# Experts of a two-layer block: rounds of up to 224 rows, and narrow turns with the rows stationary and the weights moving

## The reference, cut to what matters

```python
def _swiglu(h, w_in, w_out):
    a, b = jnp.split(h @ w_in, 2, axis=-1)
    return (jax.nn.silu(a) * b) @ w_out

def _moe(h, router, w_in, w_out):          # h 512 x 1024, w_in 1024 x 2816, w_out 1408 x 1024, 8 of each
    logits = (h @ router).astype(F32)
    top_v, top_i = lax.top_k(logits, MOE_TOP_K)                    # MOE_TOP_K = 2
    top_w = jax.nn.softmax(top_v, axis=-1)
    gates = jnp.sum(jax.nn.one_hot(top_i, MOE_EXPERTS, dtype=F32) * top_w[..., None], axis=-2).astype(h.dtype)
    return sum(gates[..., e, None] * _swiglu(h, w_in[e], w_out[e]) for e in range(MOE_EXPERTS))
```

## Time and profile before

| | |
|---|---|
| runs | 2776.82, 2778.45, 2781.89 us; median 2778.45 |
| profiled execution, its own time | 2776.83 us |
| its span | 2775.0 us |
| PE busy / DVE / ACT / POOL over the span | 96% / 36% / 24% / 18% |
| a narrow turn (2159.15 to 2221.26 us) | 62.11 us |
| a wide turn (2283.38 to 2400.87 us) | 117.49 us |
| after TensorE's last matmul | 14.90 us |

### The profile page before, as it was taken

The page is one execution under the profiler, slowest core; times in us unless marked ns, Lnnn a source line. Parts: engine busy times, 40 slices in busy tenths (PEclk is TensorE's granted clock), DMA queues, the critical chain, the costliest instruction groups (busy, mean ns, idle before and its releaser), DMA issues. The chain is left out here.

```text
span 2775.0 us, 46116 instructions
## 1 busy us (share of the span) xinstructions
PE 2658.9 (96%) x18752; PEld 1775.5 (64%) x18753; DVE 1003.8 (36%) x2301; ACT 666.8 (24%) x1408; POOL 502.2 (18%) x465
## 2 busy tenths in 40 slices
PE   6999999889999999999999999999988999999997
PEld 3555555555555555556677667766647788677784
DVE  2344454337767763113444444444440110010100
ACT  3344444221222210115232333232111110110110
POOL 0111111022223314222223222321100010000000
PEclk8999999989999999999999999999998999999999
DMA  7224223213333332201001100110239995684831
GB/s 243 67 71 127 68 66 87 82 46 102 110 116 111 106 111 69 63 23 32 20 14 33 32 24 10 32 32 1 70 122 368 334 308 175 204 264 154 267 94 30
DMA packets 321858, 297.60 MB, mean 107 GB/s; under 512 B 5920, under 2 KB 285600, under 8 KB 321568
## 3 DMA queue, kind: packets, MB, share of 16 engines
q1 hardware_dynamic: 315648, 273.17, 32.4%
q0 software_dynamic: 4896, 17.83, 2.5%
q10 hardware_dynamic: 1152, 4.19, 0.4%
HBM read 281.01 MB, written 12.58 MB: 106 GB/s over the span
## 5 line engine op out<-in xcount | busy, mean ns | idle before, releaser
L1762 PE MATMUL bank<-work,weight_ring 128*128 128x128 f32 (+1 forms) x2048 | 317.7, 317 | 1.0 <-ACT work L1812 1.0
L2228 PE MATMUL bank<-hidden,weight_ring 128*128 128x512 f32 (+1 forms) x768 | 308.7, 536 | 1.8 <-ACT work L2572 1.8
L1762 PEld LDWEIGHTS bank<-work,weight_ring 128*128 128x128 f32 x2048 | 291.0, 192 | 24.9 <-ACT work L1812 5.7
L655 PE MATMUL bank<-weight_ring,hidden 128*128 128x384 f32 x760 | 266.7, 495 | 4.8 <-ACT work L799 4.6
L1283 PE MATMUL bank<-hidden,weight_ring 128*128 128x384 f32 x704 | 238.1, 492 | 5.0 <-ACT hidden L426 5.0
L1429 DVE SCALAR_TENSOR_TENSOR weight_ring<-weight_ring,silu_c 128x256 f32<-128x256 f32 x308 | 213.7, 735 | 5.5
L655 PEld LDWEIGHTS bank<-weight_ring,hidden 128*128 128x128 f32 x760 | 138.0, 191 | 109.0 <-ACT work L799 16.6
L1283 PEld LDWEIGHTS bank<-hidden,weight_ring 128*128 128x128 f32 x704 | 133.1, 192 | 93.7 <-issue 7.0
L2228 PEld LDWEIGHTS bank<-hidden,weight_ring 128*128 128x128 f32 x768 | 134.9, 190 | 82.4 <-issue 68.1
L1934 DVE TENSOR_TENSOR work<-work,bank 128x128 f32<-128x128 f32 (+1 forms) x88 | 29.7, 338 | 423.7 <-ACT work L1818 423.7
L1283 PE MATMUL bank<-weight_ring 128*128 128x384 f32 x528 | 182.1, 495 | 0.3 <-DVE work L1437 0.3
(11 more groups left out here) (372 smaller groups left out, 3741.0 us busy)
## 6 DMA issues: line engine op xcount, KB each, us to landing
weight_ring<-in_moe_w_in SPq DMA_DIRECT2D x64, 1024.0 KB, 10.3
weight_ring<-in_ada_w SPq DMA_DIRECT2D x38, 1024.0 KB, 5.3
weight_ring<-in_ffn_w_in SPq DMA_DIRECT2D x44, 512.0 KB, 4.9
hidden<-in_moe_w_out SPq DMA_DIRECT2D x8, 2816.0 KB, 10.6
residual<-in_moe_w_out SPq DMA_DIRECT2D x8, 2816.0 KB, 16.1
work<-in_moe_w_in SPq DMA_DIRECT2D x16, 1024.0 KB, 8.8
weight_ring<-in_na_w_qkv SPq DMA_DIRECT2D x24, 512.0 KB, 8.0
weight_ring<-in_gdn_w_qkv SPq DMA_DIRECT2D x24, 512.0 KB, 5.3
```

The lines of the kernel that those rows point to most:

```text
L655: mm = nc.tensor.matmul(m.psum[6][:, 0:3 * P], m.H[:, k, t * P:(t + 1) * P], weights(u)[:, k, :], start=(k == 0), stop=(k == KD - 1))
L1762: mm = nc.tensor.matmul(B[c % 4][:, ab * HALF:ab * HALF + N], w[:, ab, k, (c % 2) * P:(c % 2 + 1) * P], XG[:, k, 0:N], start=(k == 0), sto ...
L2228: mm = nc.tensor.matmul(B[b][:, c0:c0 + t1 - t0], W[:, s, k, :], m.H[:, k, t0:t1], start=(k == 0), stop=(k == KD - 1))
```

## The change

A round has up to 224 rows in two blocks of 128 and 96, in place of two of 128. The wide turn keeps its form with N = 224. Gather, scatter, transposes, `pick`, `take_rows` and the second product take 96 rows in the second block. 512 tokens now make up to three rounds, so the table has 24 turns (and one) and its last round is cut at the end of the tokens; the extra rounds run if an expert has more than 224 rows.

The narrow turn's first product is turned round. For each slab of 256 hidden units (the last 128), 8 matmuls have the rows `XG[:, k, 0:128]` stationary and move both halves of the slab, 512 columns in two runs of 256. The result has rows on partitions. ScalarE and VectorE work on it a slab at a time, into `sa`, in place. TensorE then transposes each 128 columns back (`turn_back`, eleven a turn, in banks 6 and 7), one slab late, and VectorE copies them to `GT` (`take`).

```diff
-    TURNS = 2 * EXPERTS
     HALF = 2 * P
+    BACK = 96
+    ROUND = P + BACK
+    ROUNDS = -(-LAT // ROUND)
+    TURNS = ROUNDS * EXPERTS
+    BLOCK = (P, BACK)
...
-        with eng.If(most > HALF):
+        with eng.If(most > ROUND):
...
             def scatter(b):
-                nc.gpsimd.indirect_dma_start(out=m.out[0], out_offset=bass.IndirectOffsetOnAxis(ap=row_now[:, b:b + 1], axis=0),
-                                             in_=YS[:, b, :], in_offset=None, compute_op=ALU.add).then_inc(scattered[b], 16)
+                r = slice(0, BLOCK[b])
+                nc.gpsimd.indirect_dma_start(out=m.out[0], out_offset=bass.IndirectOffsetOnAxis(ap=row_now[r, b:b + 1], axis=0),
+                                             in_=YS[r, b, :], in_offset=None, compute_op=ALU.add).then_inc(scattered[b], 16)
...
# TensorE
-            def turn(it, nb):
-                N = nb * P
+            def turn_rows(it, nb):
+                N = sum(BLOCK[0:nb])
...
+            def wide(it):
+                nb = 2
+                N = sum(BLOCK)
+                turn_rows(it, nb)
                 for c in range(EK):
...
+                second(it, nb, ready)
+                pe.sem_inc(turned, SLABS)
+
+            def narrow(it):
+                turn_rows(it, 1)
+
+                def turn_back(j):
+                    pe.wait_ge(gated, it * EK + min(2 * j + 2, EK))
+                    if j < 2:
+                        pe.wait_ge(sum_out, it * 2 + 2)
+                    else:
+                        pe.wait_ge(taken, it * SLABS + j - 1)
+                    for n in range(chunks(j)):
+                        mm = nc.tensor.transpose(B[TURN_BANKS[j % 2]][:, n * P:(n + 1) * P], sa[:, j % 2, n * P:(n + 1) * P], ident)
+                    mm.then_inc(turned, 1)
+
+                for j in range(SLABS):
+                    pe.wait_ge(w_in[j], it * 32 + 32)
+                    if j >= 4:
+                        pe.wait_ge(gated, it * EK + 2 * (j - 4) + 2)
+                    n = width(j)
+                    w = in_slab(j)[:, 0:KD * 2 * n].rearrange("p (s k n) -> p s k n", k=KD, s=2)
+                    for k in range(KD):
+                        if j == 0 and k % 2 == 0:
+                            pe.wait_ge(x_out, it * KD + k + 2)
+                        mm = nc.tensor.matmul(B[j % 4][:, 0:2 * n].rearrange("p (s n) -> p s n", s=2), XG[:, k, 0:P], w[:, :, k, :],
+                                              start=(k == 0), stop=(k == KD - 1))
+                    mm.then_inc(product, chunks(j))
+                    if j == 2:
+                        pick(it + 2)
+                    if j:
+                        turn_back(j - 1)
+
+                def ready(k):
+                    if k == 4:
+                        turn_back(SLABS - 1)
+                    if k % 2 == 0:
+                        pe.wait_ge(taken, it * SLABS + k // 2 + 1)
+
+                second(it, 1, ready)
...
# ScalarE, narrow
+                for j in range(SLABS):
+                    n = width(j)
+                    act.wait_ge(product, it * EK + EK + min(2 * j + 2, EK))
+                    if j >= 2:
+                        act.wait_ge(turned, it * SLABS + j - 1)
+                    nc.scalar.activation(sa[:, j % 2, 0:n], B[j % 4][:, 0:n], ACT.Silu).then_inc(silu_ok, chunks(j))
...
# VectorE, setting up
+            LAST = ROUND * (ROUNDS - 1)
+            for r in range(1, ROUNDS):
+                nc.vector.tensor_scalar(of(2, r), of(2, 0), float(-ROUND * r), None, ALU.add).then_inc(rank_ok, 1)
+            nc.vector.tensor_scalar(late, of(2, 0), float(LAST), None, ALU.is_ge).then_inc(rank_ok, 1)
+            dve.wait_ge(rank_ok, 15)
+            nc.vector.tensor_tensor(of(1, ROUNDS - 1), of(1, ROUNDS - 1), late, ALU.mult).then_inc(rank_ok, 1)
+            nc.vector.tensor_scalar(place, late, float(-LAT), float(LAT), ALU.mult, ALU.add).then_inc(rank_ok, 1)
+            dve.wait_ge(rank_ok, 17)
+            nc.vector.tensor_tensor(of(2, ROUNDS - 1), of(2, ROUNDS - 1), place, ALU.add).then_inc(rank_ok, 1)
...
# VectorE, narrow
+                def take(j):
+                    dve.wait_ge(turned, it * SLABS + j + 1)
+                    nc.vector.tensor_copy(GT[:, 2 * j:2 * j + chunks(j), 0:P], B[TURN_BANKS[j % 2]][:, 0:width(j)].rearrange("p (n t) -> p n t", n=chunks(j)))\
+                        .then_inc(taken, 1)
+
+                for j in range(SLABS):
+                    n = width(j)
+                    dve.wait_ge(silu_ok, it * EK + min(2 * j + 2, EK))
+                    nc.vector.tensor_tensor(sa[:, j % 2, 0:n], sa[:, j % 2, 0:n], B[j % 4][:, n:2 * n], ALU.mult).then_inc(gated, chunks(j))
+                    if j == 0:
+                        next_turn(it)
+                    if j:
+                        take(j - 1)
+                    if j == 3:
+                        next_rows(it)
+                take(SLABS - 1)
+                weighted(it, 1)
```

More of the change, by code:

```diff
@@ L1573, in experts, with chunks, rounds @@
     Y_BANKS = ((5, 6), (7, 5))
+    TURN_BANKS = (6, 7)
     def width(s):
         return HALF if s < SLABS - 1 else P
-    def rounds(eng, turn):
+    def chunks(j):
+        return width(j) // P
+    def rounds(eng, wide, narrow):
         eng.wait_ge(table_ok, 2)
@@ L1584, in rounds @@
             with eng.If(mine > P):
-                turn(e, 2)
+                wide(e)
             with eng.Else():
-                turn(e, 1)
-        with eng.If(most > HALF):
+                narrow(e)
+        with eng.If(most > ROUND):
             with eng.Fori(EXPERTS, TURNS) as it:
-                turn(it, 2)
+                wide(it)
     with nc.Block() as block:
@@ L1680, in _ @@
                 turn(e)
-            with pool.If(most > HALF):
+            with pool.If(most > ROUND):
                 with pool.Fori(EXPERTS, TURNS) as it:
@@ L1766, in turn @@
                         pick(it + 2)
[L1767 to L1779, removed]
@@ L1783, in _ @@
+            rounds(pe, wide, narrow)
         @block.scalar
@@ L1813, in turn, with wide @@
                                              scale=m.MODA[:, 1, 1, 2 * j + k, 0:1]).then_inc(x_out, 1)
+            def wide(it):
+                N = sum(BLOCK)
+                turn_rows(it, 2)
                 for c in range(EK):
@@ L1818, in turn, with narrow @@
                     nc.scalar.activation(sa[:, c % 2, 0:N], B[c % 4][:, 0:N], ACT.Silu).then_inc(silu_ok, 1)
-            rounds(act, turn)
+            def narrow(it):
+                turn_rows(it, 1)
+                for j in range(SLABS):
[4 more added lines that the diff above has]
+                    nc.scalar.activation(sa[:, j % 2, 0:n], B[j % 4][:, 0:n], ACT.Silu).then_inc(silu_ok, chunks(j))
+            rounds(act, wide, narrow)
         @block.vector
@@ L1880, in _ @@
             tok = const(m, C_TOK, 4).unsqueeze(2).broadcast_to([P, 4, EXPERTS])
-            for r in range(2):
+            for r in range(ROUNDS):
                 nc.vector.tensor_copy(of(0, r), tok).then_inc(rank_ok, 1)
@@ L1927, in _, with next_turn, next_rows, weighted @@
             dve.wait_ge(gain_out, 2)
[L1928 to L1944, removed]
+            dve.wait_ge(rank_ok, 19)
+            def next_turn(it):
+                    dve.wait_ge(picked, it + 1)
+                    nc.vector.tensor_copy(now.unsqueeze(2), table[:, :, bass.ds(it + 1, 1), :]).then_inc(now_ok, 1)
+                    dve.wait_ge(now_ok, it + 2)
+                    one_hots()
+            def next_rows(it):
+                    dve.wait_ge(idx_kept, it + 1)
+                    for b in range(2):
+                        dve.wait_ge(gathered[b], it * 16 + 16)
+                    take_rows(it + 2)
+            def weighted(it, nb):
                 for half in range(2):
@@ L1957, in turn, with wide, narrow @@
                 keep_gates(it + 2)
-            rounds(dve, turn)
+            def wide(it):
+                N = sum(BLOCK)
+                for c in range(EK):
+                    dve.wait_ge(silu_ok, it * EK + c + 1)
+                    nc.vector.tensor_tensor(GT[:, c, 0:N], sa[:, c % 2, 0:N], B[c % 4][:, HALF:HALF + N], ALU.mult).then_inc(gated, 1)
+                    if c == 1:
+                        next_turn(it)
+                    if c == 7:
+                        next_rows(it)
+                dve.sem_inc(taken, SLABS)
+                weighted(it, 2)
+            def narrow(it):
+                def take(j):
[7 more added lines that the diff above has]
+                    if j == 0:
+                        next_turn(it)
+                    if j:
+                        take(j - 1)
+                    if j == 3:
+                        next_rows(it)
+                take(SLABS - 1)
+                weighted(it, 1)
+            rounds(dve, wide, narrow)
 class Steps:
```

79 lines of the change are left out of this document (51 added, 28 removed).

## The result

The changed kernel takes 2737.89 us (median of four runs, 2737.49 to 2745.18) beside 2777.64 us for the kernel before. The ratio is 0.9866, with a 95% interval from 0.9849 to 0.9883: 37.2 us less, between 32.5 and 41.9. The forecast was 2744.3 us, 34.1 us less. The profiled execution took 2745.18 us, the longest of the four; its span is 2743.2 us.

The account below looks back on a forecast made before the run. TensorE's gapless instructions were taken to bound the experts' turns. Wide turns 28.0, narrow turns 5.6 and tail 0.5 us sum to 34.1 us less: 2778.45 to 2744.3 us, own range 2738 to 2749, with near rivals 2737 to 2754.

Parts of the forecast that it names:

- Wide turns, term 28.0 us: Three wide turns: first product with 224 columns takes 66.95 us in place of 76.30; 28.0 us less in all.
- Narrow turns, term 5.6 us: Five narrow turns: first product 2.62 us less, transposes back 1.5 us more; net 1.1 us a turn, 5.6 us.
- The first turn: First of the five narrow turns, counted like the others: 1.1 us less.
- Waits, weights, clock: Narrow turns: new waits covered, weights hidden; rivals of DMA bounding (chance 0.05) and clock falling to 1.2 GHz (0.02).
- One sign: Sign to look for ahead of the experts' turns: the first turn starts at 2095.6 as now.
- covered: Narrow turns: transposes one slab late wait for nothing; without that cover 1 us a slab would show.
- Two runs of a moving operand: Rival, narrow first product: moving operand in two runs of 256 is slow; 514 ns a record loses 34 us; chance 0.05.
- The tail, term 0.5 us: After the last turn: second scatter has 96 rows in place of 128; 0.5 us less.
- The sum: Whole kernel: 28.0 + 5.6 + 0.5 = 34.1 us less, median 2744.3 us.

Follow-up runs that it names:

- the changed kernel again: No edit: the changed kernel run once more beside the kernel before; 2741.72 us, ratio 0.9868.
- the kernel of three widths: Changed kernel plus a third kind of turn, N = 192, for experts with 129 to 192 rows; 2726.25 us, ratio 0.9825.

## Why the prediction was right

**Wide turns, term 28.0 us.** Right. A record of 224 columns is 30.37/160 = 189.8 ns (forecast 190.2). The first product is 67.14 us (66.95), the second 37.77, the start 1.57. A turn is 9.54 us shorter, 28.6 us in three; the surplus over 9.35 is the 0.2 us of `pick`, which the account of changed parts left out, though `pick` was named there.

**Narrow turns, term 5.6 us.** Right in the mechanism and in its net size for the four later turns: long records at 429.4 ns, eleven transposes for 1.27 us (four pairs of 0.22, one behind `pick` of 0.28, and one of 0.11), no gap. With `pick` each of them is 1.32 us shorter, without it 1.10, for a forecast of 1.12. But two errors cancel in that. The first product takes 38.07 us and not 37.81, so it wins 2.36 us and not 2.62: its first 32 records take 14.00 us where 32 x 429.4 ns is 13.74. So of the 0.9 us that the forecast put down to TensorE's wait for ScalarE, only some 0.6 went away. And the transposes cost 1.27 us and not 1.5. By the figure of the Trainium skill ("TensorE: Matmul & The Clock Gate", Part 4: PE-mode transpose) of 275 ns each they would have cost 3.0 us. As the duration of one it agrees with the 273 ns of the earlier trace rows; as a price in a stream the runs here don't bear it out, there it is 110 ns, also two at a time; on an idle engine a pair took 0.44 us.

**The first turn** was mis-sized. It lasts 62.94 us (2098.47 to 2161.41) against 63.54, so 0.6 us less and not 1.1. TensorE comes out of its wait of 11.8 us for the gather at a clock of 0.50, and stays there for about 5 us, so the long records begin at the 1.2 GHz level: 15.30 us for two slabs where later turns take 14.00, 1.30 more. The kernel before has this slow start as well, as its stretches show (the records in the second column, the clock in the third from the right):

```profile
2097.60:2099.60 2.00, 2.00 (x11) 2.00 (x11) 0.00 (x0) 1.98 (x6) 0.00 (x0) 0.50 1.11 346
2099.60:2101.60 2.00, 2.00 (x15) 2.00 (x15) 0.00 (x0) 0.94 (x1) 0.00 (x0) 0.70 1.17 305
2101.60:2103.60 2.00, 2.00 (x21) 2.00 (x20) 0.29 (x1) 0.28 (x1) 0.00 (x0) 1.00 1.06 256
```

Yet its first 192 records took 23.03 us, only 0.57 more than in later turns. In its trace they start 213 ns apart at the low clock, without a gap, whereas in a later turn TensorE waits for ScalarE at the start, some 0.6 us in all. At the low clock TensorE is slow enough not to wait. So the wait that the turned form takes away in later turns wasn't there in the first to be taken away. The size of this term isn't sure to 0.5 us: the same two slabs take between 14.21 and 15.55 us in the profiles with turned narrow turns, by how soon the clock rises.

**Waits, weights, clock.** Right. No wait for `taken`, `gated` or a slab stands in the chain; the clock is 1.00 in the turns; the DMA share is 1.07 at 342 GB/s in a narrow turn and yet nothing waits for a slab. (The forecast misread that share for the kernel before as 1.00; the earlier trace rows has 1.06.) Silu and product of a slab are done 1.1 us after it, at 2177.66 for the slab that ends at 2176.52. One sign didn't come: the first turn starts at 2098.47 and not at 2095.6, by the spread ahead of the experts. The experiment without the lag showed what stood behind "covered": 8.0 us a turn, where the forecast said 1 us a slab. The price of a cover was underestimated, because the table load, the restart of the transposes and the clock weren't in it.

**Two runs of a moving operand** cost nothing: 429.4 ns a record with two runs of 256, 429.3 with one of 512 (`w_out`).

**The tail, term 0.5 us.** One pair of profiles gives 0.15 us (14.90 to 14.75; the second scatter's landing takes 6.74 us in place of 6.91), but the tail scatters by more than that: 14.12 us in the changed kernel again, and 14.01 to 15.02 in the eight profiles with rounds of 224 rows, 14.4 in the mean, against 14.90 and 14.77 in the two with 128. By these means it is 0.4 us, near the forecast 0.5, and no single pair resolves it.

**The sum.** 4 x 1.32 + 0.60 + 3 x 9.54 + 0.15 = 34.65 us, against 34.7 us in the stage and 34.1 forecast. That the forecast comes within 0.6 us is in part luck: `pick` gave 1.7 us that no term had, and the first turn, `pick` left out, and the tail of this profile gave about 1.1 us less than their terms. The median moved by more, 37.2 us by the ratio, with an interval that holds 34.7 and 34.1. The measured 2737.89 us lies 6.4 us under the forecast, just under its own range (2738 to 2749) and within the wide one (2737 to 2754); 0.8 us of that is the kernel before, 2777.64 us in place of 2778.45. The profiles show no gain outside the stage. What spreads the starts of the first turn over 9.5 us from one execution to another lies ahead of the experts and stays open; the 2 us between stage and medians are no larger than that spread.

## What to carry to other kernels

When TensorE is busy without gaps, a change can be priced from the spacing of its records (columns, plus a few ns each), and such a price held here within 1 ns; ask next which operands are short. Turning a matmul round, so that the long side moves, won 2.4 us a turn, and the transposes back took half of it; it pays only if these come a stage late: with the lag laid open, stops of 1.2 us and more cost 8 us a turn, 43 us in all, more than the whole change brought. And fit the moving columns to the data: each 32 columns off an expert's turn were worth 9.5 us, more than all five turned narrow turns.

## What the runs showed of the hardware

- Transposes that alternate between 128-row and 64-row operands cost 0.12 to 0.14 us for each change, 3.53 us against 1.57 for sixteen; 96 rows beside 128 cost nothing.
- The granted clock can fall with no gap in TensorE's busy time. In the kernel with rounds of 192 it did so around 16 of 19 such slow starts of 3.5 to 4 us, to 0.58 and 0.57 in the 4 us behind one of 3.69 us; behind the two of 3.53 us in the kernel of three widths it stayed at 1.00. What decides between the two isn't shown.
- In the narrow turns of the changed kernel the DMA engines show a share of 1.01 and 1.07, at 315 and 342 GB/s, and no slab was waited for: here the share says that transfers were under way, not that one was late.
